# The expert products of a hybrid block: 448-column products with the two halves summed on VectorE

## Chip, cores and metric

The kernel runs on one core of one Trainium2 chip. The metric is the device time of one execution in microseconds (us).

## What is computed

One block of a hybrid network in float32 on 256 tokens of width 2048: a projection, a retention branch and an RWKV-7 branch, a gated merge, and then the layer that this change is about. It scores 16,384 experts, takes for every token 16 experts in each of 8 heads, and sums their outputs:

```
def block(args):
    xb, eb, gb = args
    ue = jnp.take(expert_u, eb, axis=0)
    act = jax.nn.gelu(jnp.einsum('nhkd,nd->nhk', ue, xb), approximate=False) * gb
    return jnp.einsum('nhk,nhkd->nd', act, jnp.take(expert_v, eb, axis=0))
...
x = x + peer(h2, peer_w_q, peer_keys_1, peer_keys_2, peer_u, peer_v)
return rms_norm(x, final_norm_w)
```

## The kernel before

224 of the 256 tokens (`DT`) are computed densely: every expert's row is multiplied with every token, and a matrix of gates `G` (128 blocks of 128 experts, by 224 tokens) is zero where an expert was not chosen. The other 32 tokens (`SPARSE`) gather their experts' rows with indirect DMAs from GpSimd and are computed on VectorE (`sparse_step`).

**Split precision.** A float32 operand is split in two parts of type fp32r: a high part (a copy on ScalarE, `hi`, L958) and a low part (raw minus high). The product is high x high, high x low activation, and low weight x high. Weights stream in as *units* of 128 x 1024, each in two halves of 512 columns. Units have four places in `raw` and two in `w_hi` and `w_lo` (`k % 2`). ScalarE makes the high part of a half when TensorE has counted `half_used` for the half four before it. The low part is made by GpSimd for the units 0 and 2 of each four (`p_split`, L1392) and by VectorE for 1 and 3 (`d_split`, L1437).

**Stage u** (64 iterations of four units, two blocks of 128 experts; `um`, L858 to L872). The two units of a block accumulate in one PSUM bank of 224 columns (bank 4 or 5). For each half: eight products of 224 columns on the high weights (high and low activation in turn, L867 and L868), then, after a wait for the low part, four on the low weights (L871). ScalarE takes Gelu from PSUM into `G` (`gelu`, L1239). VectorE picks the top 16 meanwhile, in small pieces (`pick_steps`). In the last 29 iterations (*gate turns*, i from 0 to 28) the gates are built: VectorE makes one-hot rows (`hot_e2`, `hot_e1`), ScalarE scales them (`hot_gate`, L1253), TensorE multiplies them (`gates_mm`, L879, after unit 1 and after unit 3), VectorE multiplies the result into `G` (`gate_in`, L1974) and the late Gelu results too (`late_in`, L1981). I call a half turn, two units and their gates, a *par*.

**Stage v** (64 iterations of four units; `vm`, L900 to L929). The activation of a block is split as well (ScalarE L1307, VectorE L2083, in `v_lo`), once per block, that is twice per iteration. 16 tiles of output (2048 channels) of 224 columns each stay in the eight PSUM banks, two to a bank, through the whole stage. A unit is one block and half of the output channels; again eight high products (L920) and then four low ones (L923) per half. At the end the tiles are copied to SBUF, turned (L937) and added to the residual, and the last norm follows.

The order of each engine is written out by hand: every engine runs its list in order and waits on counters. In u, VectorE and ScalarE do the work for the block before (`gelu(it - 1, ...)`) between the parts of the current one. `MAC_AT`, `DOT_AT` (when a gathered tile is used), `ADD_AT` and `FINAL_AT` are iteration numbers.

Of the kernel before, what the change touches and what calls it, by code (L numbers as in the profile page):

```python
# [102 lines left out]
def hybrid_block_kernel(nc, a):  # L103
# [4 lines left out]
    with ctx:  # L108
# [156 lines left out]
        act2 = act_both.rearrange("p c w n -> p (c w n)")[:, 0:4 * DT].rearrange("p (s w n) -> p s w n", s=2, w=2)  # L265
# [5 lines left out]
        out_T = Z(64, 80)  # L271
        part_last = small[:, 34:42].rearrange("p (t k) -> p t k", t=2)

        def v_bank(j):
            return PS[:, j // 2, (j % 2) * DT:(j % 2 + 1) * DT]

        def v_both(bank):
            return PS[:, bank, 0:2 * DT].rearrange("p (t n) -> p t n", t=2)
# [70 lines left out]
        def _(sp):  # L349
# [120 lines left out]
            def load_v(it):  # L470
                for k in range(4):
                    if isinstance(it, int) and it == 0:
                        sp.wait_ge(*split_done("u", UPAIRS - 1, k, 2))
                    else:
                        sp.wait_ge(*split_done("v", it - 1, k, 2))
                    sp.dma_start(raw[:, k, :], v_rows[ds(it * 2 + k // 2, 1), :, (k % 2) * 1024:(k % 2 + 1) * 1024]
                                 .rearrange("a e n -> e (a n)")).then_inc(S[f"raw_in{k}"], 16)
            run_loop(sp, 0, FINAL_AT, load_v)

            sp.wait_ge(S["half_used"], 2 * (V0 + 2 * 28))  # L480
            for piece in range(12):
                if piece == 8:
                    sp.wait_ge(S["rows_added"], 16 * 4)
                if piece % 2 == 0:
                    load_v(FINAL_AT + piece // 2)
                part, q = piece // 4, piece % 4
                if part == 0:
                    sp.dma_start(flat(Z(16 + 2 * q, 18 + 2 * q)),
                                 a["final_norm_w"][q * 512:(q + 1) * 512].partition_broadcast(P)).then_inc(S["fw_in"], 16)
                else:  # L490
                    tt = 2 - part
                    sp.dma_start(flat(Z(8 * tt + 2 * q, 8 * tt + 2 * q + 2)),
                                 x1_dram[tt * P:(tt + 1) * P, q * 512:(q + 1) * 512]).then_inc(S["x1_in"], 16)
            for it in range(FINAL_AT + 6, BLOCKS // 2):
                load_v(it)

            for tt in range(2):
                for h in (1, 0):
                    sp.wait_ge(*((S["normed"], 3 + tt) if h == 0 else (S["y_ready"], tt + 1)))
                    cols = slice(1024 * h, 1024 * h + 1024)  # L500
                    sp.dma_start(a["out"][0, tt * P:(tt + 1) * P, cols], flat(Z(24 + 8 * tt, 32 + 8 * tt))[:, cols]).then_inc(S["stored"], 16)
            sp.wait_ge(S["stored"], 64)
# [3 lines left out]
        def _(pe):  # L506
# [398 lines left out]
            def vm(it, k, first=False, final=False):  # L905
                b = k // 2
                if k % 2 == 0:
                    pe.wait_ge(S["act2_split"], it * 2 + (b + 1))
                for hh in range(2):
                    tiles = [(8 * (k % 2) + 4 * hh + t, slice((4 * hh + t) * P, (4 * hh + t + 1) * P)) for t in range(4)]  # L910
                    pe.wait_ge(S["unit_hi"], it * 8 + (2 * V0 + 2 * k + hh + 1))
                    for j, cols in tiles:
                        if first and j == 0:
                            pe.wait_ge(S["hot1"], 2 * GATE_TURNS)
                        if first and j in (8, 10):
                            pe.wait_ge(S[f"gelu{(j - 8) // 2}"], UPAIRS)
                        if first and j in (12, 14):
                            pe.wait_ge(S[f"gated{(j - 12) // 2}"], GATE_TURNS)
                        for w in range(2):
                            pe.matmul(v_bank(j), w_hi[:, k % 2, cols], act2[:, b, w, :], start=first and j % 2 == 0 and w == 0, stop=False)  # L920
                    pe.wait_ge(*split_done("v", it, k, hh + 1))
                    for j, cols in tiles:
                        last = pe.matmul(v_bank(j), w_lo[:, k % 2, cols], act2[:, b, 0, :], start=False, stop=final and j % 2 == 1)  # L923
                        if final and j % 2:
                            last.then_inc(S["tile_done"], 1)
                    if not final:
                        last.then_inc(S["half_used"], 1)
                    elif 2 * (k % 2) + hh > 0:
                        turn_rows(2 * (k % 2) + hh - 1)  # L929

            def turn_rows(q):

                pe.wait_ge(S["out_even"], q + 1)
                pe.wait_ge(S["out_odd"], q + 1)
                for tt in range(2):
                    for c in range(4):
                        last = pe.transpose(PS[:, 2 * q + tt, c * P:(c + 1) * P], out_T[:, 4 * q + c, tt * P:(tt + 1) * P], ident)  # L937
                    last.then_inc(S["rows_T"], 1)

            def v_pair(it, first=False, final=False):  # L940
                for k in range(4):
                    vm(it, k, first and k < 2, final and k >= 2)
            v_pair(0, first=True)
            with pe.Fori(1, BLOCKS // 2 - 1) as it:
                v_pair(it)
            v_pair(BLOCKS // 2 - 1, final=True)
            turn_rows(3)
# [3 lines left out]
        def _(act):  # L951
# [284 lines left out]
            def gelu(it, b):  # L1236

                act.wait_ge(S["half_used"], it * 8 + (2 * U0 + 4 * b + 4))
                act.activation(rowof(2 * it + b if isinstance(it, int) else it * 2 + b), PS[:, 4 + b, 0:DT], ACT.Gelu).then_inc(S[f"gelu{b}"], 1)  # L1239

            def late_gelu(i, b):

                act.wait_ge(S["half_used"], i * 8 + (2 * U0 + 8 * GATE_AT + 4 * b + 4))
                if not (isinstance(i, int) and i == 0):
                    act.wait_ge(S["late"], i * 2 + (b - 1))
                act.activation(late_out[b], PS[:, 4 + b, 0:DT], ACT.Gelu).then_inc(S[f"gelu{b}"], 1)
# [51 lines left out]
            def v_hi(it):  # L1298
                for k in range(4):
                    b = k // 2  # L1300
                    if k % 2 == 0:

                        if isinstance(it, int) and it == 0 and b == 0:
                            act.wait_ge(S["half_used"], 2 * V0 - 2)
                        else:
                            act.wait_ge(S["half_used"], it * 8 + 2 * (V0 + 2 * b - 2))
                        act.activation(act2[:, b, 0, :], rowof(2 * it + b if isinstance(it, int) else it * 2 + b), ACT.Copy).then_inc(S["act2_hi"], 1)  # L1307
                    for hh in range(2):
                        hi(it + V0 // 4, k, hh)
                    if isinstance(it, int) and it == 0 and k == 0:  # L1310
                        late_gelu(GATE_TURNS, 1)
                    if isinstance(it, int) and it == 0 and k == 1:
# [3 lines left out]
            run_loop(act, 0, EARLY // 2, v_hi)  # L1316

            act.wait_ge(S["late"], BLOCKS - EARLY)
            with act.Fori(EARLY // 2, BLOCKS // 2) as it:
                v_hi(it)  # L1320

            def odd_out(bank):
                act.wait_ge(S["tile_done"], bank + 1)
                act.activation(out_T[:, 2 * bank:2 * bank + 2, SPARSE:TOK], v_both(bank), ACT.Copy).then_inc(S["out_odd"], 1)
# [9 lines left out]
            for q in range(4):  # L1334
                odd_out(2 * q + 1)
                if q > 0:
                    square_last(0, q - 1)
                    square_last(1, q - 1)
# [12 lines left out]
        def _(pool):  # L1351
# [63 lines left out]
            for g in range(2 * UPAIRS):  # L1415
# [3 lines left out]
                if ADD_AT <= g < ADD_AT + 4:  # L1419
                    add_sparse(g - ADD_AT)  # L1420
                low_parts("u" if g < UPAIRS else "v", g % UPAIRS, U_SPLIT if g < UPAIRS else V_SPLIT, U0 // 4 + g)

# [552 lines left out]

# [212 lines left out]
```

## Time and profile before

| | |
|---|---|
| median of 3 runs | 2376.08 us (2372.18 to 2376.28) |
| profiled execution | 2374.39 us, its span 2372.6 us |
| TensorE busy | 2338.8 us, 99% of the span |
| VectorE, ScalarE, GpSimd busy | 1526.2 us, 1340.8 us, 830.7 us |
| stage u | 928.3 to 1671.0 us of the span |
| stage v | 1671.0 to 2360.1 us |
| mean granted clock of TensorE | 0.997 |

The profile gives busy time per engine, the chain of work that ended last, and groups of instructions by line with their mean duration. Products overlap in their pipeline, so an instruction's own duration (275 ns for 224 columns) says little; the distance from one start to the next is what a product costs. "Idle before" is what an engine waited for.

### The profile page before, as it was taken

The page shows a single profiled execution, that of the slowest core. Times are in us where ns is not written, and L with a number is a line of the kernel's source. Part 1 is how long each engine was busy: PE and PEld are TensorE (multiplying, and loading weights), DVE is VectorE, ACT ScalarE, POOL GpSimd, SP SyncE. Part 2 cuts the span into 40 slices and gives each one's busy share as a digit, 9 for nine tenths or more (in the row PEclk, how much of TensorE's full clock was granted, in tenths as well). Part 3 has the DMA queues.
Part 4 walks back from the last instruction along what each step waited for, and adds up shares of the span by engine and source line. Part 5 has one row for each costly group of instructions (what it writes and reads, how often), then busy time and mean ns, then how long its engine had stood idle before and what let it go on. Part 6 is the DMA issues. An engine that isn't in the chain of part 4 may idle for free.

```text
span 2372.6 us, 51129 instructions
## 1 busy us (share of the span) xinstructions
PE 2338.8 (99%) x19066; PEld 2203.6 (93%) x19066; DVE 1526.2 (64%) x2468; ACT 1340.8 (57%) x2369; POOL 830.7 (35%) x612
## 2 busy tenths in 40 slices
PE   9999999999999999999999999999999999999998
PEld 8888787978888789999999999999999999999998
DVE  5568988557566565675667877776456566666534
ACT  5456554255544545777776666666555555555555
POOL 0000201100000002445556545554556566666554
PEclk9999999999999999999999999999999999999999
DMA  7665554046666557666778766675777777777684
GB/s 215 186 195 151 160 168 152 22 128 193 194 195 215 169 182 230 193 199 220 240 260 283 255 216 233 227 242 165 259 252 248 266 248 256 260 256 262 226 256 147
DMA packets 197218, 499.52 MB, mean 211 GB/s; under 512 B 14726, under 2 KB 82824, under 8 KB 187656
## 3 DMA queue, kind: packets, MB, share of 16 engines
q1 hardware_dynamic: 187719, 430.20, 57.1%
q0 software_dynamic: 9408, 68.16, 8.2%
q8 instruction: 51, 0.84, 0.1%
q14 instruction: 40, 0.32, 0.0%
HBM read 491.98 MB, written 5.24 MB: 210 GB/s over the span
## 4 chain that ended last, share of the span: by engine, by line
PE 92%; DVE 3%; ACT 2%; DMA 1%; POOL 1%; issue 1%; SPq 0%; ACTq 0%
PE PS L920 19%; PE PS L923 10%; PE PS L518 9%; PE PS L867 9%; PE PS L868 9%; PE PS L871 9%; PE PS L561 5%; PE PS L563 5%; PE PS L562 5%; PE PS L520 4%; PE PS L511 3%; PE PS L879 2%; DVE w_lo L1437 1%; POOL big L1364 1%; DMA raw<-in_w_out 0%
## 5 line engine op out<-in xcount | busy, mean ns | idle before, releaser
L958 ACT ACTIVATE w_hi<-raw 128x512 fp32r<-128x512 f32 x1576 | 985.6, 631 | 919.9 <-PE PS L923 291.3
L1437 DVE TENSOR_TENSOR w_lo<-raw,w_hi 128x512 fp32r<-128x512 f32 x1064 | 748.3, 715 | 759.1 <-ACT w_hi L958 757.1
L1392 POOL TENSOR_TENSOR w_lo<-raw,w_hi 128x512 fp32r<-128x512 f32 x512 | 707.7, 1392 | 1095.4 <-ACT w_hi L958 1089.3
L920 PE MATMUL PS<-act_both,w_hi 128*128 128x224 f32 x4096 | 540.5, 274 | 0.0
L920 PEld LDWEIGHTS PS<-act_both,w_hi 128*128 128x128 f32 x4096 | 498.5, 192 | 0.2 <-DVE act_both L2083 0.2
L867 PE MATMUL PS<-act_both,w_hi 128*128 128x224 f32 x2048 | 489.0, 277 | 3.6 <-ACT big L1239 3.6
L868 PE MATMUL PS<-act_both,w_hi 128*128 128x224 f32 x2048 | 483.2, 274 | 0.0
L867 PEld LDWEIGHTS PS<-act_both,w_hi 128*128 128x128 f32 x2048 | 393.0, 192 | 4.3 <-issue 4.3
L868 PEld LDWEIGHTS PS<-act_both,w_hi 128*128 128x128 f32 x2048 | 393.1, 192 | 0.0
L518 PE MATMUL PS<-act_both,w_hi 128*128 128x512 f32 x1056 | 373.2, 400 | 6.9 <-DVE w_lo L1437 6.1
L923 PE MATMUL PS<-act_both,w_lo 128*128 128x224 f32 x2048 | 312.1, 275 | 0.3 <-POOL w_lo L1392 0.2
L871 PE MATMUL PS<-act_both,w_lo 128*128 128x224 f32 x2048 | 311.8, 274 | 0.0
L520 PE MATMUL PS<-act_both,w_lo 128*128 128x256 f32 x990 | 278.6, 281 | 0.0
L923 PEld LDWEIGHTS PS<-act_both,w_lo 128*128 128x128 f32 x2048 | 269.8, 192 | 0.6 <-POOL w_lo L1392 0.6
L871 PEld LDWEIGHTS PS<-act_both,w_lo 128*128 128x128 f32 x2048 | 269.8, 192 | 0.0
L518 PEld LDWEIGHTS PS<-act_both,w_hi 128*128 128x128 f32 x1056 | 197.1, 189 | 55.4 <-DVE w_lo L1437 7.9
L561 PE MATMUL PS<-w_hi,act_both 128*128 128x512 f32 x576 | 226.9, 394 | 2.5 <-DVE w_lo L1437 2.3
L563 PE MATMUL PS<-w_hi,act_both 128*128 128x512 f32 x576 | 224.2, 389 | 0.0
L562 PE MATMUL PS<-w_lo,act_both 128*128 128x512 f32 x576 | 224.2, 389 | 0.0
L520 PEld LDWEIGHTS PS<-act_both,w_lo 128*128 128x128 f32 x990 | 187.7, 190 | 1.5 <-issue 0.2
L561 PEld LDWEIGHTS PS<-w_hi,act_both 128*128 128x128 f32 x576 | 108.1, 188 | 28.0 <-DVE w_lo L1437 4.8
L563 PEld LDWEIGHTS PS<-w_hi,act_both 128*128 128x128 f32 x576 | 108.1, 188 | 22.7
(261 smaller groups left out, 1930.6 us busy)
## 6 DMA issues: line engine op xcount, KB each, us to landing
raw<-in_peer_u_t SPq DMA_DIRECT2D x256, 512.0 KB, 4.3
raw<-in_peer_v SPq DMA_DIRECT2D x256, 512.0 KB, 4.7
raw<-in_w_in SPq DMA_DIRECT2D x180, 512.0 KB, 3.8
raw<-in_w_out SPq DMA_DIRECT2D x32, 512.0 KB, 4.5
raw<-in_peer_w_q SPq DMA_DIRECT2D x32, 512.0 KB, 4.3
raw<-in_w_ret_branch SPq DMA_DIRECT2D x16, 512.0 KB, 4.4
raw<-in_w_rwkv_branch SPq DMA_DIRECT2D x16, 512.0 KB, 4.5
big<-in_x SPq DMA_DIRECT2D x2, 1024.0 KB, 5.9
```

Of the source, the lines that this page charges most:

```text
L518: last = pe.matmul(PS[:, bank, :], wh, act_both[:, kc, :, :].rearrange("p w n -> p (w n)"), start=start, stop=stop)
L520: last = pe.matmul(PS[:, bank, 0:TOK], wl, act_hi[:, kc, :], start=False, stop=False)
L561: pe.matmul(out, ah, w_hi[:, slot % 2, cols], start=first, stop=False)
L563: last = pe.matmul(out, al, w_hi[:, slot % 2, cols], start=False, stop=last_k)
L867: pe.matmul(out, w_hi[:, k % 2, cols], act_hi[:, kc, SPARSE:TOK], start=kc == 0, stop=False)
L868: pe.matmul(out, w_hi[:, k % 2, cols], act_lo[:, kc, SPARSE:TOK], start=False, stop=False)
L871: last = pe.matmul(out, w_lo[:, k % 2, cols], act_hi[:, kc, SPARSE:TOK], start=False, stop=kc == 15)
L920: pe.matmul(v_bank(j), w_hi[:, k % 2, cols], act2[:, b, w, :], start=first and j % 2 == 0 and w == 0, stop=False)
L923: last = pe.matmul(v_bank(j), w_lo[:, k % 2, cols], act2[:, b, 0, :], start=False, stop=final and j % 2 == 1)
L958: act.activation(w_hi[:, slot % 2, hh * 512:(hh + 1) * 512], raw[:, slot, hh * 512:(hh + 1) * 512], ACT.Copy).then_inc(S["unit_hi"], 1)
L1392: pool.tensor_tensor(w_lo[:, k % 2, cols], raw[:, k, cols], w_hi[:, k % 2, cols].bitcast(f32), ALU.subtract).then_inc(S["p_split"], 1)
L1437: dve.tensor_tensor(w_lo[:, slot % 2, cols], raw[:, slot, cols], w_hi[:, slot % 2, cols].bitcast(f32), ALU.subtract).then_inc(S[done], 1)
```

## The change

The two products of 224 columns on the same high weights become one of 448 (high and low activation side by side). Their results lie beside each other in PSUM, so a sum is needed: VectorE's `tensor_reduce` over the pair. In u that is `usum`, one for each of the 128 blocks, ahead of Gelu, which now reads and writes SBUF. In v, 448 columns take a whole bank for each tile, so only eight of the 16 tiles fit: stage v runs twice over all 128 blocks, each time for half of the channels (`h` = 0, 1), with a drain between (`last_units`, `sum_tile`, `odd_out`); a unit is then one block, and its activation is split in both passes. The long and the short product of each piece of 128 columns come in turn, and the wait for the low part stands ahead of both. Some iteration numbers move with it, and the last rows are turned in another grouping (`rows_of`).

```diff
             def um(it, k):
-                out = PS[:, 4 + k // 2, 0:DT]
+                bank = 4 + k // 2
                 for hh in range(2):
                     if k % 2 == 0 and hh == 0:
-                        wait_past(pe, S[f"gelu{k // 2}"], it)
-                    pe.wait_ge(S["unit_hi"], it * 8 + (2 * U0 + 2 * k + hh + 1))
+                        wait_past(pe, S[f"gelu{k // 2}"], 2 * it - 1)
+                    pe.wait_ge(*split_done("u", it, k, hh + 1))
                     chunks = [((k % 2) * 8 + 4 * hh + c, slice((4 * hh + c) * P, (4 * hh + c + 1) * P)) for c in range(4)]
                     for kc, cols in chunks:
-                        pe.matmul(out, w_hi[:, k % 2, cols], act_hi[:, kc, SPARSE:TOK], start=kc == 0, stop=False)
-                        pe.matmul(out, w_hi[:, k % 2, cols], act_lo[:, kc, SPARSE:TOK], start=False, stop=False)
-                    pe.wait_ge(*split_done("u", it, k, hh + 1))
-                    for kc, cols in chunks:
-                        last = pe.matmul(out, w_lo[:, k % 2, cols], act_hi[:, kc, SPARSE:TOK], start=False, stop=kc == 15)
+                        pe.matmul(pair_bank(bank), w_hi[:, k % 2, cols], act_both[:, kc, :, SPARSE:TOK], start=kc == 0, stop=False)
+                        last = pe.matmul(PS[:, bank, 0:DT], w_lo[:, k % 2, cols], act_hi[:, kc, SPARSE:TOK], start=False, stop=kc == 15)
                     last.then_inc(S["half_used"], 1)
...
             def late_gelu(i, b):
-                act.wait_ge(S["half_used"], i * 8 + (2 * U0 + 8 * GATE_AT + 4 * b + 4))
...
-                act.activation(late_out[b], PS[:, 4 + b, 0:DT], ACT.Gelu).then_inc(S[f"gelu{b}"], 1)
+                act.wait_ge(S[f"gelu{b}"], 2 * i + (2 * GATE_AT + 1))
+                act.activation(late_out[b], late_out[b], ACT.Gelu).then_inc(S[f"gelu{b}"], 1)
...
+            def usum(it, b, late=True):
+                dve.wait_ge(S["half_used"], it * 8 + (2 * U0 + 4 * b + 4))
+                dve.tensor_reduce(late_out[b] if late else G[:, 2 * it + b, :], summed(4 + b), AX.X, ALU.add).then_inc(S[f"gelu{b}"], 1)
...
                 for par in range(2):
+                    usum(i + (GATE_AT - 1), par, not first)
                     if not first:
                         gate_in(i - 1, par)
...
+            def v_lo(h, it):
+                g = UPAIRS + h * (BLOCKS // 4) + it
+                for k in range(4):
...
+                    dve.wait_ge(S["act2_hi"], it * 4 + (h * BLOCKS + k + 1))
+                    dve.tensor_tensor(act2[:, k, 1, :], rowof(4 * it + k), act2[:, k, 0, :].bitcast(f32), ALU.subtract).then_inc(S["act2_split"], 1)
...
-MAC_AT = [66 + 8 * t // 5 for t in range(PICK_TILES)]
+MAC_AT = [66 + 8 * t // 5 for t in range(17)] + [100 + 5 * t // 4 for t in range(PICK_TILES - 17)]
...
-IDS_AT, ADD_AT, FINAL_AT = 15, 118, 54
+IDS_AT, ADD_AT, FINAL_AT = 15, 119, 24
```

The order of instructions shows what moves. TensorE, one half of a unit of stage u, before:

```order
L867 MATMUL PS<-act_both,w_hi 128x224 [waits s_unit_hi]
L868 MATMUL PS<-act_both,w_hi 128x224
L867 MATMUL PS<-act_both,w_hi 128x224
L868 MATMUL PS<-act_both,w_hi 128x224
L871 MATMUL PS<-act_both,w_lo 128x224 [waits s_p_split]
L871 MATMUL PS<-act_both,w_lo 128x224 x3
```

and changed, where L876 is the long product and L877 the short one:

```order
L876 MATMUL PS<-act_both,w_hi 128x448 [waits s_p_split]
L877 MATMUL PS<-act_both,w_lo 128x224
L876 MATMUL PS<-act_both,w_hi 128x448
L877 MATMUL PS<-act_both,w_lo 128x224
```

Eight and four products of 224 columns have become four of 448 and four of 224, and the half waits for its low part before its first product and not before its ninth. (Of the eight high products the first piece shows four.)

VectorE, one par of a gate turn with a gathered tile, before (L1437 are the low parts, L2002 the gathered tile):

```order
L1974 TENSOR_TENSOR big<-PS,big 128x128x4 [waits s_late,s_g_mm1]
L1986 TENSOR_TENSOR onehot<-PS,extra 128x512 [waits s_g_mm1]
L1989 TENSOR_TENSOR cst<-PS,extra 128x512
L1981 TENSOR_TENSOR big<-big,extra 128x224 [waits s_gated1,s_gelu1]
L1437 TENSOR_TENSOR w_lo<-raw,w_hi 128x512 [waits s_unit_hi] x2
L2002 ISA big,vec<-big,inv 128x1024
```

and changed (L1485 and L2055 are the low parts and the gathered tile there):

```order
L2027 TENSOR_REDUCE extra<-PS 128x224 [waits s_half_used]
L2022 TENSOR_TENSOR big<-PS,big 128x128x4 [waits s_late,s_g_mm1]
L2039 TENSOR_TENSOR onehot<-PS,extra 128x512 [waits s_g_mm1]
L2042 TENSOR_TENSOR cst<-PS,extra 128x512
L2034 TENSOR_TENSOR big<-big,extra 128x224 [waits s_gated1,s_gelu1]
L1485 TENSOR_TENSOR w_lo<-raw,w_hi 128x512 [waits s_unit_hi] x2
L2055 ISA big,vec<-big,inv 128x1024
L2027 TENSOR_REDUCE cst<-PS 128x224 [waits s_half_used]
```

The sum of a block stands at the head of a par, behind the low parts and the gathered tile of the par before. ScalarE, changed, from the last high part of one par to the next par (L1277 is the late Gelu, L1284 the scaling of the one-hot rows):

```order
L990 ACTIVATE w_hi<-raw 128x512 [waits s_half_used]
L1277 ACTIVATE extra<-extra 128x224 [waits s_gelu1]
L1284 ACTIVATE cst<-cst,extra 128x128 [waits s_hot0]
L1284 ACTIVATE cst<-cst,extra 128x128 x3
L990 ACTIVATE w_hi<-raw 128x512 [waits s_half_used,s_raw_in2]
```

The order is that of before; the Gelu's wait was on TensorE's counter `half_used` and is now on the sum (`s_gelu1` counts sums and Gelus).

## Rows read from the trace of the kernel before

**Rows 1.** The page: busy time of the engines, and the chain that ended last by engine and line.

```profile
PE 2338.8 (99%) x19066; PEld 2203.6 (93%) x19066; DVE 1526.2 (64%) x2468; ACT 1340.8 (57%) x2369; POOL 830.7 (35%) x612
...
PE 92%; DVE 3%; ACT 2%; DMA 1%; POOL 1%; issue 1%; SPq 0%; ACTq 0%
```

**Rows 2.** Windows: u without gates, gate turns, v, the end.

```profile
928.40:1313.00 384.60, 380.98 (x3394) 380.27 (x3394) 261.31 (x649) 283.42 (x427) 204.74 (x156) 1.00 0.72 231
1313.00:1662.00 349.00, 349.00 (x3128) 349.00 (x3127) 257.43 (x414) 219.06 (x501) 174.40 (x129) 1.00 0.67 223
1671.00:2354.00 683.00, 682.73 (x6110) 682.21 (x6109) 375.09 (x451) 358.02 (x641) 400.89 (x290) 1.00 0.73 248
2354.00:2372.60 18.60, 8.03 (x71) 7.57 (x70) 11.26 (x21) 9.66 (x24) 4.70 (x2) 0.81 0.28 113
```

**Rows 3.** Chain in order of time (start, us, what), stage v, one half of a unit.

```profile
2345.84 0.45 PE PS L923 x4
2346.29 0.89 PE PS L920 x8
2347.18 0.45 PE PS L923 x4
```

**Rows 4.** The same view in the query projection: 512 and 256 columns in turn.

```profile
879.26 0.23 PE PS L518
879.49 0.12 PE PS L520
879.61 0.24 PE PS L518
```

**Rows 5.** Timeline of TensorE: products of 512 columns alone; and the chain's turns of 128 columns.

```profile
599.84 0.39 PE L563 MATMUL PS<-w_hi,act_both 128*128 128x512 f32 x1
600.07 0.39 PE L561 MATMUL PS<-w_hi,act_both 128*128 128x512 f32 x1
600.29 0.39 PE L562 MATMUL PS<-w_lo,act_both 128*128 128x512 f32 x1
...
2357.88 0.87 PE PS L937 x8
```

**Rows 6.** Timeline of a gate turn, TensorE's two groups of gate products.

```profile
1453.12 1.06 PE L879 MATMUL PS<-cst 128*128 128x128 f32 x8
1459.37 1.06 PE L879 MATMUL PS<-cst,onehot 128*128 128x128 f32 x8
```

**Rows 7.** Timeline of the same turn, VectorE.

```profile
1454.59 0.68 DVE L1974 TENSOR_TENSOR big<-PS,big 128x512 f32<-128x512 f32 x1
...
1456.38 1.42 DVE L1981 TENSOR_TENSOR big<-big,cst 128x224 f32<-128x224 f32 x1
...
1460.23 0.69 DVE L1437 TENSOR_TENSOR w_lo<-raw,w_hi 128x512 fp32r<-128x512 f32 x1 [0.65 <-ACT w_hi L958]
1460.84 1.22 DVE L2002 CUSTOM_DVE_ANT_0 inv<-inv 128x1024 f32<-128x1024 f32 x1
1461.99 0.08 DVE L2002 DVE_READ_ACCUMULATOR2_ANT vec<- 128x1 f32 x1
1461.99 0.68 DVE L1974 TENSOR_TENSOR big<-PS,big 128x512 f32<-128x512 f32 x1
```

**Rows 8.** Timeline of the same turn, ScalarE and GpSimd.

```profile
1459.57 0.63 ACT L958 ACTIVATE w_hi<-raw 128x512 fp32r<-128x512 f32 x1 [0.71 <-PE PS L871]
1460.11 0.34 ACT L1246 ACTIVATE extra<-PS 128x224 f32<-128x224 f32 x1
1460.35 1.27 ACT L1253 ACTIVATE cst<-cst,extra 128x128 f32<-128x128 f32 x4
...
1456.26 2.69 POOL L1392 TENSOR_TENSOR w_lo<-raw,w_hi 128x512 fp32r<-128x512 f32 x2 [2.10 <-ACT w_hi L958]
```

**Rows 9.** One line's instructions, min/median/max ns: a PSUM copy of 448, and the activation's low part.

```profile
L2104 DVE COPY big<-PS x4: 617/625/625, 2354.3 to 2359.9; 128x448 f32<-128x448 f32 x4
...
L2083 DVE TENSOR_TENSOR act_both<-big,act_both x128: 327/392/1487, 1669.2 to 2348.9; 128x224 fp32r<-128x224 f32 x128
```

**Rows 10.** Timeline of ScalarE in u without gates.

```profile
1100.18 1.28 ACT L1239 ACT_TABLE_LOAD   x1
1101.47 0.36 ACT L1239 ACTIVATE big<-PS 128x224 f32 x1
1101.72 1.14 ACT L958 ACTIVATE w_hi<-raw 128x512 fp32r<-128x512 f32 x2
```

**Rows 11.** Who waited for whom in stage v: us in total, times, longest; and a weight load's landing.

```profile
ACT w_hi L958 <- PE PS L923: 291.3, 464, 1.1
...
ACT w_hi L958 <- DMA raw<-in_peer_v: 31.3, 22, 1.9
...
raw<-in_peer_v SPq DMA_DIRECT2D x256, 512.0 KB, 4.7
```

More of the change, by code:

```diff
@@ L909, in vm @@
+            def vm(h, it, k, first=False):
+                pe.wait_ge(S["act2_split"], it * 4 + (h * BLOCKS + k + 1))
                 for hh in range(2):
-                    tiles = [(8 * (k % 2) + 4 * hh + t, slice((4 * hh + t) * P, (4 * hh + t + 1) * P)) for t in range(4)]
-                    pe.wait_ge(S["unit_hi"], it * 8 + (2 * V0 + 2 * k + hh + 1))
+                    tiles = [(4 * hh + t, slice((4 * hh + t) * P, (4 * hh + t + 1) * P)) for t in range(4)]
+                    pe.wait_ge(*split_done("v", it + h * (BLOCKS // 4), k, hh + 1))
@@ L912, in vm @@
                     for j, cols in tiles:
[L913 to L929, printed above, removed]
@@ L931, in turn_rows @@
-            def turn_rows(q):
-                pe.wait_ge(S["out_even"], q + 1)
-                pe.wait_ge(S["out_odd"], q + 1)
-                for tt in range(2):
+                        if first:
+                            bank_free(h, j)
+                        pe.matmul(pair_bank(j), w_hi[:, k % 2, cols], act2[:, k], start=first, stop=False)
+                        last = pe.matmul(PS[:, j, 0:DT], w_lo[:, k % 2, cols], act2[:, k, 0, :], start=False, stop=False)
+                    last.then_inc(S["half_used"], 1)
@@ L938, in turn_rows, with last_units @@
                     last.then_inc(S["rows_T"], 1)
[L940 to L947, printed above, removed]
+            def last_units(h):
+                it = BLOCKS // 4 - 1
+                for j in range(8):
+                    cols, halves = slice(j * P, (j + 1) * P), j // 4 + 1
+                    for k in (2, 3):
+                        if j == 0:
+                            pe.wait_ge(S["act2_split"], h * BLOCKS + 4 * it + k + 1)
+                        if j % 4 == 0:
+                            pe.wait_ge(S["unit_hi"], 2 * (V0 + h * BLOCKS + 4 * it + k) + halves)
+                        pe.matmul(pair_bank(j), w_hi[:, k % 2, cols], act2[:, k], start=False, stop=False)
+                    for k in (2, 3):
+                        if j % 4 == 0:
+                            pe.wait_ge(*split_done("v", it + h * (BLOCKS // 4), k, halves))
+                        last = pe.matmul(PS[:, j, 0:DT], w_lo[:, k % 2, cols], act2[:, k, 0, :], start=False, stop=k == 3)
+                        if k == 2 and j % 4 == 3:
+                            last.then_inc(S["half_used"], 1 if j == 3 else 3)
+                    last.then_inc(S["tile_done"], 1)
+                    if h == 1 and j in (2, 4, 6):
+                        turn_rows((j - 2) // 2)
+                if h == 1:
+                    turn_rows(3)
@@ L950, in _, with v_blocks @@
+            for h in range(2):
+                def v_blocks(it, first=False, final=False):
+                    for k in range(2 if final else 4):
+                        vm(h, it, k, first and k == 0)
+                    if final:
+                        last_units(h)
+                v_blocks(0, first=True)
+                with pe.Fori(1, BLOCKS // 4 - 1) as it:
+                    v_blocks(it)
+                v_blocks(BLOCKS // 4 - 1, final=True)
         @block.scalar
@@ L1315, in v_hi @@
                         sqrt_table()
-            run_loop(act, 0, EARLY // 2, v_hi)
+                    if start and h == 1 and k == 0:
+                        odd_out(7)
+            run_loop(act, 0, EARLY // 4, lambda it: v_hi(0, it))
             act.wait_ge(S["late"], BLOCKS - EARLY)
[L1319 to L1324, printed above, removed]
+            with act.Fori(EARLY // 4, BLOCKS // 4) as it:
+                v_hi(0, it)
+            run_loop(act, 0, BLOCKS // 4, lambda it: v_hi(1, it))
             def square_last(tt, q):
@@ L2032, in u_step @@
                     sparse_step(it, k // 2)
+                if unit >= 4 and k % 2 == 0:
+                    usum(it - 1, k // 2, False)
             def scale_rows(w):
@@ L2076, in _ @@
                 gate_turn(i)
[L2077 to L2089 removed]
+            usum(BLOCKS // 2 - 1, 0)
```

202 lines of the change are left out of this document (121 added, 81 removed).

## The prediction

> **What bounds the kernel now.** I read the page first. TensorE is busy 99% of the span and the chain that ended last runs on it for 92% [rows 1], so the kernel is as long as TensorE's list. The windows then say where the change acts: 384.6 us of stage u without gates, 349.0 us of gate turns, 683.0 us of stage v, TensorE busy throughout [rows 2]. The change touches these three. What is read next is the distance between products, since overlapping durations do not show it.
>
> One half of a unit takes 0.89 us for its eight high products and 0.45 us for its four low ones [rows 3], so 1.34 us for twelve, 0.112 us each, and three products, the work on one piece of 128 weight columns, take 0.335 us. The turns, with 128 columns, take 0.87 us for eight, 0.109 us each [rows 5]. So a product of 224 columns costs hardly more than one of 128: at this width it is not the columns that set the distance but what comes with every product, the load of its own weights.
>
> **What a long product costs.** No product of 448 columns is in the trace. The nearest rows are 512 and 256 columns in turn, 0.235 and 0.118 us, 0.353 for the pair [rows 4], and 512 alone, 0.227 us [rows 5]. The bounds for 448 with 224:
> - Below, in proportion to the columns: 0.353 x 672 / 768 = 0.309 us. That gains 0.026 on 0.335.
> - Above, the short one as in rows 4 (0.118) and the long one less 64 columns at the 0.4 to 0.46 ns per column of rows 4 and 5, 0.207: 0.325 us, a gain of 0.010.
> - I take 0.207 + 0.112 = 0.319 us, because the short product is most like those of 224 columns in rows 3, and no product there or in rows 5 comes in less than 0.109. Gain 0.016 us.
>
> There are 128 blocks x 16 pieces in u and as many in v, 4,096 pieces: 66 us of TensorE's time (41 to 106). A half is then 4 x 0.319 = 1.28 us instead of 1.34, and an iteration of eight halves 10.21 instead of 10.72, 0.51 less.
>
> The Trainium skill (TensorE: Matmul & The Clock Gate, section LDWEIGHTS) gives a weight load as the columns divided by 1.2, 107 ns for 128; the 109 to 112 ns of rows 3 and 5 agree. The same page (Back-to-back issue gap) gives an isolated product as N/2.4 + 2.5 ns. That would make the long one 189 ns and the pair with a load of 107 come to 296, a gain of 160 us over the pieces; but by it 512 columns would take 216 ns, and the trace has 227.
>
> **What the sum adds, and what now stands behind it.** A copy of 448 columns from PSUM takes VectorE 0.62 us [rows 9]; I take that for the sum. Next to instructions of 0.68 us that follow at 0.60 us [rows 7] it occupies some 0.6.
>
> *Gate turns* (28 with gates, 56 pars; a par now takes 1459.37 - 1453.12 = 6.25 us [rows 6]). TensorE alone would need 4 x 1.28 + 0.90 = 6.01. But ScalarE's late Gelu waits for a sum that VectorE issues behind the low parts and the gathered tile of the par before. The loop from one last high part to the next: low part 0.61 (1460.23 to 1460.84), gathered tile 1.15 (to 1461.99) [rows 7], sum 0.62, Gelu 0.24 and scaling 1.27 [rows 8], four high parts at 0.57 to 0.63, which TensorE does not hold up then, 2.4 [rows 8, 10]: 6.3 us. With handovers 6.35. It needs no TensorE, so where a gathered tile is used (20 of the 29 turns, by `DOT_AT`) it sets the par: 6.35 instead of 6.25, 40 x 0.10 = +4 us. In the other 16 pars, without the 1.15, the loop is 5.2 and TensorE sets 6.01: -4 us. To that comes a collision: VectorE's `late_in` took 1.42 us where GpSimd's low part had begun just before (1456.26 and 1456.38 [rows 7, 8]). The sum pushes `late_in` to about 1.8 us behind itself, and GpSimd starts its low part some 2.2 us behind it, so now one waits, now the other; I put down 5 us. Gate turns: +5, all in all nothing won. This is the first place where the gain stays out.
>
> *u without gates* (35 iterations): -0.51 x 35 = -18 us. Here the loop after the last high part of an iteration is low part 0.69, perhaps a gathered tile 1.2, a piece of the top-16 work of 1 to 1.8, sum 0.62, and then ScalarE's table load 1.28 and Gelu 0.36 [rows 10], which start only when the sum is done, high part 0.6, low part 0.7. That is 7.2 us at most against six halves less one high part, 7.0 us, until TensorE needs it. So it bites in the six iterations that have both a gathered tile and top-16 work, and more weakly elsewhere: 5 us, and 3 us for weights that land late, which the wait ahead of the first product no longer forgives. -18 + 8 = -10.
>
> *Stage v* (64 iterations): -0.51 x 64 = -33 us. Added are 128 activation splits: ScalarE 0.37 us, VectorE 0.33 to 1.49 [rows 9]. VectorE is busy 375 of 683 us and ScalarE 358 [rows 2]; with 128 x 0.9 = 115 and 128 x 0.37 = 47 us more both stay under 75% of the shorter stage, and they are split a unit ahead, so they cost nothing while these engines keep two microseconds of lead. The wait ahead costs lead: the high part of a half starts when the half four before it is done, and its low part from GpSimd is there 0.1 + 0.6 + 1.4 = 2.1 us later; TensorE wants it after three halves, 3.8 us. Spare is 1.7 us, where today the low part had 3.9 + 0.9 - 2.1 = 2.8. ScalarE waited for weights 22 times, 1.4 us in the mean, 1.9 at most [rows 11], and the window in which a load must land (4.7 us in the middle) shrinks by 0.4 us. I put down 5 us for it, 1 for the drain between the two passes (the first half of the new pass waits for the last tiles), 2 for the end, where eight sums of 0.62 us lie beside the adds. -33 + 8 = -25.
>
> The exclusive port behind the spread of rows 9 is in the Trainium skill (SBUF — State Buffer, Who interferes with whom): VectorE with two SBUF inputs and a GpSimd instruction that reads SBUF block each other for a whole instruction, a `tensor_reduce` never does. The maximum of 1487 ns against a minimum of 327 agrees. It speaks against the 128 new splits, and not against the sums; by it the sum would change only if the splits' lead were gone.
>
> **Sum.** -10 + 5 - 25 = -30 us on 2374.4, so 2344; the median of the runs shown lies 1.7 above the profiled execution, so 2346.
>
> **Rivals.**
> - *Columns alone set the distance* (0.309 us a piece). For it: rows 4 are nearly in proportion (0.235 to 0.118). Against: rows 5 and 3, where 128 columns cost what 224 do. u without gates -32 + 9, gate turns as above but 16 pars at 5.84 (-7 + 9), v -54 + 12 = -42, so -63 and 2313 us. Chance 0.23.
> - *The lead is worth as much as the gain.* If each late load shows in full and there are twice as many, 44 x 1.4 = 62 us is more than v gains; halved, it takes 25 to 30 us: 2372 us, no change or little. For it: the lead of 1.7 us is under the longest wait of 1.9 [rows 11]. Against: the mean is under it, and VectorE's units have 0.7 us more. Chance 0.18.
> - *Slower: ScalarE's list hangs on the sum in every gate par.* If `late_in` meets GpSimd each time, it takes 1.42 instead of 0.38 [rows 7], the low parts come 1.0 us later, and the loop is 7.4 us in the 40 pars with a tile. That is +46 us against -35 from the rest: 2387 us. It decides from a mean par of 6.25 + 35/56 = 6.87 us on. For it: the loop already fills the par by my count. Against: the trace shows the short and the long `late_in` both. Chance 0.17.
> - *The change doesn't do what it says.* The order shows the 448-column products, the sums and the waits as written, so I give it 0.02.
>
> **Chances.** My case 0.40, and the rest as said. A measurement of this kernel tells about 0.2%, 4.8 us, from no change. The first two cases are faster, of the third about half: 0.74. Within 0.2%: 0.08. Slower: the fourth and a little of the third, 0.18. The range must reach into the first and the last rival: 2308 to 2380.
>
> **What the changed profile would show.** The pair of L876 and L877 at 0.319 us, 0.309 or 0.325 decides between the first two cases. The gate products' groups 6.35 us apart in turns with a tile and 6.0 without. ScalarE's waits for VectorE's L2027 in gate turns, of the order of a microsecond each. TensorE idle, now next to nothing in u and v, by some 20 us, in the low parts' name. I would be wrong if a pair took 0.33 us or more, if the sum took over a microsecond, or if TensorE stood in stage v for more than the 22 late loads.

## The result and the profile after

| | before | changed |
|---|---|---|
| median | 2376.08 us (2372.18 to 2376.35, 5 runs) | 2391.24 us (2387.59 to 2396.62, 5 runs) |
| span of the profiled execution | 2372.6 us | 2389.2 us |
| TensorE busy | 99% | 96% |
| VectorE busy | 1526 us | 1801 us |
| mean granted clock | 0.997 | 0.996 |

The change is slower: ratio 1.0071, 95% interval 1.0059 to 1.0083. I had forecast 2346 us, in a range of 2308 to 2380.

The page of the changed kernel, busy time and the chain, against [rows 1]:

```profile
PE 2290.7 (96%) x14970; PEld 2059.2 (86%) x14970; DVE 1801.1 (75%) x2731; ACT 1355.7 (57%) x2497; POOL 856.6 (36%) x616
...
PE 62%; DVE 20%; ACT 8%; issue 4%; DMA 2%; POOL 2%; ACTq 1%; SPq 0%; DVEq 0%
```

The chain was 92% TensorE. Now a fifth of it is VectorE, and ScalarE has 8%. The windows, cut at the same places as in [rows 2] (u without gates, gate turns, v, the end; the columns are busy time of TensorE's products, its loads, VectorE, ScalarE, GpSimd):

```profile
929.50:1306.50 377.00, 359.48 (x2250) 335.39 (x2248) 294.97 (x715) 276.21 (x422) 206.09 (x155) 1.00 0.72 234
1306.50:1699.40 392.90, 357.42 (x2237) 320.33 (x2238) 331.32 (x470) 204.42 (x505) 186.96 (x129) 1.00 0.55 197
1710.00:2366.00 656.00, 642.17 (x4064) 607.60 (x4063) 533.82 (x582) 395.29 (x772) 411.38 (x295) 1.00 0.78 260
2366.00:2389.20 23.20, 10.21 (x69) 8.78 (x67) 14.64 (x27) 8.43 (x22) 4.90 (x3) 0.80 0.26 90
```

From the starts of the products the stages come out as follows. The span grew by 16.6 us, which is the sum of the differences within a microsecond:

| stage | before | changed | difference | forecast |
|---|---|---|---|---|
| ahead of stage u | 928.4 | 929.5 | +1.1 | 0 |
| u without gates, 35 iterations | 381.8 | 377.0 | -4.8 | -10 |
| the other 29 iterations, with the gate turns | 360.2 | 403.4 | +43.2 | +5 |
| v, first to last long product | 688.3 | 664.8 | -23.5 | -27 |
| the end | 13.2 | 14.1 | +0.9 | +2 |

The products themselves did what they should. The chain in order of time, stage v, a long product (L930) and a short one (L931) in turn, against [rows 3, 4]:

```profile
1730.54 0.21 PE PS L930
1730.75 0.10 PE PS L931
1730.85 0.21 PE PS L930
1731.06 0.10 PE PS L931
1731.16 0.21 PE PS L930
```

0.62 us for two pieces (one long product and one short), and over all pieces the medians of the distances are 0.213 and 0.101 us in v, 0.211 and 0.104 in u. From the start of one half to the next, where nothing stalls, it is 1.253 us for four pieces, against 1.340 before. A piece takes 0.313 us, a little less than my 0.319, and an undisturbed iteration 10.03 us where it took 10.72 in v and 10.76 in u.

The loss is in the gate turns. One par of the changed kernel follows, in the timelines of ScalarE, VectorE and GpSimd, to be held against [rows 7, 8] (L2027 is the sum, L1277 the late Gelu, L1284 the scaling, L990 a high part, L1485 and L1434 low parts, L2055 the gathered tile):

```profile
1443.67 0.40 ACT L1277 ACTIVATE cst<-cst 128x224 f32<-128x224 f32 x1 [3.75 <-DVE cst L2027]
1443.97 1.27 ACT L1284 ACTIVATE cst<-cst,extra 128x128 f32<-128x128 f32 x4
1445.14 2.17 ACT L990 ACTIVATE w_hi<-raw 128x512 fp32r<-128x512 f32 x4
1451.06 0.39 ACT L1277 ACTIVATE extra<-extra 128x224 f32<-128x224 f32 x1 [3.74 <-DVE extra L2027]
```

```profile
1443.03 0.61 DVE L2027 TENSOR_REDUCE cst<-PS 128x224 f32<-128x448 f32 x1
...
1445.36 0.37 DVE L2034 TENSOR_TENSOR big<-big,cst 128x224 f32<-128x224 f32 x1
1446.83 2.51 DVE L1485 TENSOR_TENSOR w_lo<-raw,w_hi 128x512 fp32r<-128x512 f32 x2 [1.10 <-ACT w_hi L990]
1449.26 1.21 DVE L2055 CUSTOM_DVE_ANT_0 big<-big,inv 128x1024 f32<-128x1024 f32 x1
...
1450.41 0.61 DVE L2027 TENSOR_REDUCE extra<-PS 128x224 f32<-128x448 f32 x1
```

```profile
1445.84 2.95 POOL L1434 TENSOR_TENSOR w_lo<-raw,w_hi 128x512 fp32r<-128x512 f32 x2 [3.04 <-ACT w_hi L990]
```

From sum to sum it is 7.38 us (1443.03 to 1450.41). ScalarE stands 3.7 us in each par for the sum; then it issues four high parts in a row, for which it used to wait one by one on TensorE. GpSimd takes its two at once, 1445.84 to 1448.79. VectorE's two low parts start in this time, at 1446.83, and take 2.51 us together, against 0.69 each in [rows 7]. Taken one by one they are 0.82 and 1.77 us, and GpSimd's two are 1.27 and 1.73 us. The times fit engines that take turns: VectorE's first gets in between GpSimd's two, and its second gets through only when GpSimd's second is done. Tile, sum and Gelu wait behind them. It is the same in nearly every par. VectorE's low parts over all gate turns, before and changed (one line's instructions, min/median/max ns):

```profile
L1437 DVE TENSOR_TENSOR w_lo<-raw,w_hi x112: 674/693/718, 1316.4 to 1660.3; 128x512 fp32r<-128x512 f32 x112
```

```profile
L1485 DVE TENSOR_TENSOR w_lo<-raw,w_hi x112: 678/1066/1775, 1306.5 to 1693.8; 128x512 fp32r<-128x512 f32 x112
```

TensorE, which needs 5.9 us for a par (experiment 2), is in none of these steps. The waits of the whole stretch of gate turns (us in total, times, longest):

```profile
ACT cst L1277 <- DVE cst L2027: 94.8, 28, 3.8
ACT extra L1277 <- DVE extra L2027: 92.1, 27, 3.8
```

Theory A, after the result, is this loop with the collision of low parts in it. Theory B: VectorE has too much work in a gate turn, so that the sum costs as work and not as a wait. Theory C: the wait for the low part ahead of the long products costs.

### The profile page after: what moved, and what is told of

Same layout as the page of the kernel before. It is cut to its first block, busy times and chain, and to the rows that moved or that the text cites. A ratio compares the mean times of both kernels' runs of the same rounds, so it can differ in the third digit from the quotient of the medians.

```text
span 2389.2 us, 42796 instructions
## 1 busy us (share of the span) xinstructions
PE 2290.7 (96%) x14970; PEld 2059.2 (86%) x14970; DVE 1801.1 (75%) x2731; ACT 1355.7 (57%) x2497; POOL 856.6 (36%) x616
## 4 chain that ended last, share of the span: by engine, by line
PE 62%; DVE 20%; ACT 8%; issue 4%; DMA 2%; POOL 2%; ACTq 1%; SPq 0%; DVEq 0%
PE PS L930 15%; PE PS L527 9%; DVE w_lo L1485 9%; PE PS L931 7%; PE PS L570 5%; PE PS L572 5%; PE PS L571 5%; ACT w_hi L990 5%; PE PS L529 4%; PE PS L876 4%; PE PS L520 3%; DVE big L2055 2%; PE PS L877 2%; ACT cst L1284 2%; POOL w_lo L1434 1%
## 5 line engine op out<-in xcount | busy, mean ns | idle before, releaser
L990 ACT ACTIVATE w_hi<-raw 128x512 fp32r<-128x512 f32 x1576 | 957.9, 628 | 656.5 <-PE PS L931 238.9
L1434 POOL TENSOR_TENSOR w_lo<-raw,w_hi 128x512 fp32r<-128x512 f32 x512 | 739.9, 1466 | 1073.3 <-ACT w_hi L990 1073.0
L1485 DVE TENSOR_TENSOR w_lo<-raw,w_hi 128x512 fp32r<-128x512 f32 x1064 | 801.2, 774 | 396.7 <-ACT w_hi L990 393.2
L876 PE MATMUL PS<-act_both,w_hi 128*128 128x448 f32 x2048 | 664.2, 379 | 53.1 <-POOL w_lo L1434 40.7
L930 PE MATMUL PS<-act_both,w_hi 128*128 128x448 f32 x2016 | 635.4, 376 | 13.8 <-DVE act_both L2147 7.4
L877 PE MATMUL PS<-act_both,w_lo 128*128 128x224 f32 x2048 | 543.2, 265 | 0.0
L931 PE MATMUL PS<-act_both,w_lo 128*128 128x224 f32 x2016 | 532.1, 264 | 0.0
L876 PEld LDWEIGHTS PS<-act_both,w_hi 128*128 128x128 f32 x2048 | 383.8, 187 | 111.8 <-POOL w_lo L1434 73.1
L930 PEld LDWEIGHTS PS<-act_both,w_hi 128*128 128x128 f32 x2016 | 378.1, 188 | 48.0 <-POOL w_lo L1434 13.3
L877 PEld LDWEIGHTS PS<-act_both,w_lo 128*128 128x128 f32 x2048 | 390.1, 190 | 0.0
L931 PEld LDWEIGHTS PS<-act_both,w_lo 128*128 128x128 f32 x2016 | 384.6, 191 | 0.0
L2147 DVE TENSOR_TENSOR act_both<-big,act_both 128x224 fp32r<-128x224 f32 x256 | 279.8, 1113 | 102.9 <-ACT act_both L1345 102.9
L527 PEld LDWEIGHTS PS<-act_both,w_hi 128*128 128x128 f32 x1056 | 197.1, 189 | 55.3 <-DVE w_lo L1485 7.9
L529 PEld LDWEIGHTS PS<-act_both,w_lo 128*128 128x128 f32 x990 | 187.8, 190 | 1.5 <-issue 0.2
L571 PEld LDWEIGHTS PS<-w_lo,act_both 128*128 128x128 f32 x576 | 108.2, 188 | 22.4 <-issue 0.5
```

Source lines behind the costliest of these rows:

```text
L527: last = pe.matmul(PS[:, bank, :], wh, act_both[:, kc, :, :].rearrange("p w n -> p (w n)"), start=start, stop=stop)
L529: last = pe.matmul(PS[:, bank, 0:TOK], wl, act_hi[:, kc, :], start=False, stop=False)
L571: pe.matmul(out, ah, w_lo[:, slot % 2, cols], start=False, stop=False)
L876: pe.matmul(pair_bank(bank), w_hi[:, k % 2, cols], act_both[:, kc, :, SPARSE:TOK], start=kc == 0, stop=False)
L877: last = pe.matmul(PS[:, bank, 0:DT], w_lo[:, k % 2, cols], act_hi[:, kc, SPARSE:TOK], start=False, stop=kc == 15)
L930: pe.matmul(pair_bank(j), w_hi[:, k % 2, cols], act2[:, k], start=first, stop=False)
```

## Experiments

All are made from the changed kernel. Times are medians with their ratio to the kernel before on the same chip.

**1. The sum ahead of the gathered tile, in gate turns.**

```diff
                 for par in range(2):
-                    usum(i + (GATE_AT - 1), par, not first)
+                    if first and par == 0:
+                        usum(GATE_AT - 1, 0, False)
...
                             u_lo(i + GATE_AT, k)
+                    if par == 0:
+                        usum(i + (GATE_AT - 1), 1, not first)
+                    else:
+                        usum(i + GATE_AT, 0)
                     sparse_step(i + GATE_AT, par)
...
-            usum(BLOCKS // 2 - 1, 0)
```

> The change with, in gate turns, the sum of a block moved ahead of the gathered tile on VectorE (low parts, sum, tile instead of low parts, tile, sum). Theory A (a loop through low part, tile 1.15 us, sum, Gelu, scaling, four high parts and GpSimd's two low parts sets the par at 7.38 us): the 1.15 us leaves the loop, pars with a tile fall to about 6.3 us, 40 x 1.1 = 44 us gained, about 2347 us; the tile now fills time in which VectorE waited 1.1 us. Theory B (VectorE has too much work in gate turns: the sum counts as work, wherever it stands): no change against the changed kernel, 2391 us. Theory C (the wait for the low part ahead of the long products is what costs): no change, 2391 us.

Measured: 2359.07 us, ratio 0.9932 (0.9916 to 0.9949); the mean distance between gate products fell from 7.04 to 6.45 us. 32 us of the expected 44 came, with no work taken away. A sum that costs as work, and a wait ahead of the long products, would both have stayed. So B and C are out for the most part, and VectorE's order matters.

**2. The late Gelu behind the next unit's high parts.**

```diff
-                    if k == 1:
-                        if not (isinstance(i, int) and i == 0):
-                            late_gelu(i - 1, 1)
-                        if not last:
-                            hot_gate(i, 0)
-                    if k == 3:
-                        late_gelu(i, 0)
-                        if not last:
-                            hot_gate(i, 1)
+                    elif k % 2 == 0:
+                        late_gelu(i - 1, k // 2)
+                    if k % 2 and not last:
+                        hot_gate(i, k // 2)
...
+                        late_gelu(GATE_TURNS, 0)
```

> The change with, in gate turns, ScalarE's late Gelu moved behind the next unit's two high parts; all engines do the same work. Theory A: ScalarE no longer holds the high parts of unit 0 and 2 back for the sum, GpSimd's low parts start earlier and TensorE sets the par at 4 x 1.26 + 0.90 = 5.9 to 6.1 us; 40 pars x 1.3 + 16 x 0.3 = 57 us gained, about 2335 us, faster than the kernel before. Theory B (VectorE's work, about 6.3 us in a par with a tile): little gained, 2380 to 2391 us. Theory C: no change, 2391 us.

Measured: 2326.57 us, ratio 0.9799 (0.9782 to 0.9815). Two gate-product groups in succession, timeline of TensorE of this kernel:

```profile
1443.24 1.06 PE L885 MATMUL PS<-cst,onehot 128*128 128x128 f32 x8
1449.14 1.06 PE L885 MATMUL PS<-cst 128*128 128x128 f32 x8
```

and its windows, gate turns and v:

```profile
1305.00:1642.00 337.00, 337.00 (x2282) 323.73 (x2281) 305.07 (x475) 224.90 (x507) 163.28 (x133) 1.00 0.70 233
1643.00:2308.00 665.00, 650.23 (x4120) 614.83 (x4118) 541.78 (x594) 397.35 (x777) 410.58 (x295) 1.00 0.76 255
```

All 55 distances are 5.9 us and TensorE is busy for all of the 337 us, with VectorE at 305, as many instructions as ever. The only thing moved is the late Gelu in ScalarE's list, once in each par. That shows the loop of A and refutes B: 63 of the 64.7 us between this kernel and the changed one are in the gate iterations (403.4 to 340.6). GpSimd's pair takes 2.55 us there and meets `late_in` (0.9 to 1.3 us), for which TensorE does not wait, and not the low parts (0.68 us each). What the collision is worth within the loop is not shown by this run but by experiments 5 and 6.

**3. The low part waited for behind the long products.**

```diff
                     for kc, cols in chunks:
                         pe.matmul(pair_bank(bank), w_hi[:, k % 2, cols], act_both[:, kc, :, SPARSE:TOK], start=kc == 0, stop=False)
+                    pe.wait_ge(*split_done("u", it, k, hh + 1))
+                    for kc, cols in chunks:
                         last = pe.matmul(PS[:, bank, 0:DT], w_lo[:, k % 2, cols], act_hi[:, kc, SPARSE:TOK], start=False, stop=kc == 15)
```

and the same in v; ahead of the long products stands the wait for the high part.

> The change with the low part waited for only behind the four long products of a half, then the four short ones, in u and v (but for the last units of a pass). Theory A: gate turns stay at 7.38 us a par (the loop has no TensorE in it); the stalls of u without gates (about 10 us) and of v (about 15 us) shrink by half or more: 2378 us, if the products cost the same in this order. Theory C: gate turns recover too, 2335 to 2350 us. Theory B: no change, 2391 us. Products grouped by kind: 0.314 us for a long and a short one if the order does not matter.

Measured: 2392.02 us, ratio 1.0075 (1.0057 to 1.0092), the changed kernel's time. The par is 7.07 us in the mean, u without gates 377.7 us, v 2.0 us shorter. C is out as the cause of the loss: the gate turns did not recover. But two things cancel outside them. Four long products took 0.82 us and four short ones 0.44 in v, 1.260 us for a half where it is 1.253 in turn, and an undisturbed iteration of u took 10.13 us and not 10.03. By these distances the grouped order costs some 7 us in u without gates and v together (an estimate). What is left of these two stages beyond their undisturbed halves fell by 3 and by 6 us. So the wait ahead of both products costs some 8 us, of A's side expectation of 13, and this edit pays nearly as much for the order.

**4. Stage v alone.** Stage u as in the kernel before: `um`, `gelu`, `late_gelu` and `late_in`'s count taken from there, `usum` out.

> Stage u as in the kernel before (three products of 224 columns, Gelu from PSUM, no sums), stage v as changed. Theories A and B: v alone gains about 24 us, so 2352 us; everything lost is in u. Theory C: v pays for its wait too and gains less than 10 us: 2366 us or more.

Measured: 2355.13 us, ratio 0.9913 (0.9889 to 0.9937). Its u took 381.8 and 360.2 us, as before, its v 669.0 us, within 5 of the changed kernel's. So v gains some 20 us by itself, and all that was lost was lost in u.

**5. GpSimd reads nothing.** From the first gate turn on GpSimd fills the low parts of its units with zeros, so the low parts of half the weights are left out.

```diff
+                        if m >= U0 // 4 + GATE_AT:
+                            pool.memset(w_lo[:, k % 2, cols].bitcast(f32), 0.0).then_inc(S["p_split"], 1)
+                            continue
                         pool.tensor_tensor(w_lo[:, k % 2, cols], raw[:, k, cols], w_hi[:, k % 2, cols].bitcast(f32),
```

> The change, but from the first gate turn on GpSimd fills its units' low parts with zeros instead of subtracting, so the low parts of half the expert weights are left out; it reads no SBUF. Theory A with a collision (VectorE's low part stands until both of GpSimd's are done, which is the 1.0 us that the prediction missed in the loop): a par with a tile falls from 7.38 to about 6.2 us, and in v the gathered tiles of 3 to 4 us fall to 1.3 and the stalls of about 2 us at some iterations with them. Rival (the loop is that long for the order alone): 7.3 us still.

Measured: 2314.61 us in one timing. The loop is still there, ScalarE still waits for the sum, but the par is 5.9 us mostly and 6.2 at most, and v takes 648.1 us, 16.7 less than in the changed kernel. The gathered tiles in v, of the changed kernel and of this one (one line's instructions, min/median/max ns):

```profile
L2062 DVE SCALAR_TENSOR_TENSOR big<-inv,vec,big x42: 1268/1273/3965, 1744.4 to 2268.1; 128x1024 f32<-128x1024 f32 x42
```

```profile
L2065 DVE SCALAR_TENSOR_TENSOR big<-inv,vec,big x42: 1275/1279/1282, 1684.4 to 2191.2; 128x1024 f32<-128x1024 f32 x42
```

The memsets are also quicker (two in 1.05 us against 2.95), so this alone does not tell reads from time.

**6. GpSimd writes slowly.** As 5, in 16 pieces for each half.

```diff
-                            pool.memset(w_lo[:, k % 2, cols].bitcast(f32), 0.0).then_inc(S["p_split"], 1)
+                            for n in range(16):
+                                last = pool.memset(w_lo[:, k % 2, hh * 512 + 32 * n:hh * 512 + 32 * n + 32].bitcast(f32), 0.0)
+                            last.then_inc(S["p_split"], 1)
```

> As e9_gpsimd_reads_nothing (low parts of GpSimd's units left out, zeros in their place), but the zeros are written in 16 pieces for each half, so that GpSimd takes about as long as it does to subtract or longer, and still reads no SBUF. Theory A (VectorE's two-input instructions are held while GpSimd reads): VectorE's low parts stay at 0.69 us, the gathered tiles of v at 1.28, the par well under 7.38 us although GpSimd is as slow. Rival (GpSimd's time, not its reads, made the loop long): the par goes back to 7 us or more, the low parts of VectorE to 1.3 in the mean.

Measured: 2319.61 us in one timing. The two halves took GpSimd 1.98 us, twice as long as in 5 and still less than when it subtracts, so the test is not as sharp as meant. VectorE, with GpSimd under way from 1443.73 to 1445.71:

```profile
1444.74 0.69 DVE L1490 TENSOR_TENSOR w_lo<-raw,w_hi 128x512 fp32r<-128x512 f32 x1 [1.10 <-ACT w_hi L990]
1445.76 0.69 DVE L1490 TENSOR_TENSOR w_lo<-raw,w_hi 128x512 fp32r<-128x512 f32 x1 [0.33 <-ACT w_hi L990]
```

```profile
1443.73 1.98 POOL L1436 MEMSET w_lo<- 128x32 f32 x32 [3.04 <-ACT w_hi L990]
```

The first low part began in the middle of GpSimd's writes and took its 0.69 us, and all 64 tiles of v took 1.28 us. The mean par is 6.03 us, 6.19 at most, and v took 649.1 us. In these runs an overlap with a GpSimd that writes costs VectorE nothing, and an overlap with one that reads holds it back. The Trainium skill (SBUF — State Buffer, Who interferes with whom) says just this of an instruction with two SBUF inputs; the 0.69 us here and the 2.51 us for two above agree.

**7. The Gelu a unit later in all of u.** As 2, and in `u_blocks` the Gelu stands at `k % 2` and not at `k % 2 == 0`.

> As e2_gelu_behind_high_parts, and in u without gates too ScalarE's Gelu stands one unit later (behind the high parts of units 1 and 3, not 0 and 2). Theory A (a wait for the sum in ScalarE's list is what costs in all of u): u without gates falls from 375 us towards 35 x 10.03 = 351, at least 10 us gained on e2: 2316 us or less. Theory D (there it is VectorE's order, low parts behind top-16 work and tile, that holds the products up): no more than 3 us gained.

Measured: 2317.89 us, ratio 0.9761 (0.9745 to 0.9778). u without gates went from 375.2 us in experiment 2 to 366.8 us, 8.4 and not 24: a third was ScalarE's wait, the rest is not. The iterations that stay long are single ones (12.6 us at the 25th, 10.8 to 11.2 from the 28th on).

**8. The sum directly behind the low parts in all of u.** As 7, with `usum` ahead of the tile and the top-16 work.

> As e6, and the sum stands directly behind VectorE's low parts and ahead of the gathered tile and the top-16 work in all of u. Theory A: little beyond e6, since the wait is gone already, 0 to 4 us. Theory D: a gain beyond e6 as TensorE waits for a bank until its sum is done: 5 us or more. Gate turns stay at 5.9 us a par by both.

Measured: 2325.97 us, ratio 0.9799 (0.9783 to 0.9816), slower than experiment 7 by 8 us, all of it in u without gates (374.9 us). Both theories expected no loss. The two traces point to the same collision: in u without gates eight gathered tiles took 1.8 to 2.2 us, where one did in 7, and in the iteration that grew most, from 10.1 to 14.2 us, VectorE's two low parts took 3.43 us together, having started 0.06 us behind a pair of GpSimd's. No further run was made to show it.

**9. The low wait once more, without the loop.** 7 and 3 together.

> As e6_gelu_late_everywhere (no wait for the sum in front of the high parts), with the four long products of a half ahead of the wait for its low part, as in e4. Theory A: with the loop gone the lead of a half is 1.7 us and the order of the wait matters only at late loads, 0 to 6 us gained on e6 or nothing, 2312 to 2319 us. Theory C (the wait ahead of both is a cost of its own, hidden in e4 by the loop): 10 us or more gained on e6.

Measured: 2324.89 us, ratio 0.9787 (0.9770 to 0.9803), 7 us over experiment 7 by the medians, with intervals that just touch. The two effects of experiment 3 are here too: a par takes 5.96 us for 5.91 and an undisturbed iteration of u 10.13 for 10.03, while the stalls of u without gates and of v are each some 3 us less. To wait late behind grouped products gains nothing in this kernel, with the loop or without it. An order that waits late and still takes the products in turn was not tried.

**10. The gathered tile ahead of the low parts in v.** As 7, `sparse_step` behind the splits of units 0 and 2.

> As e6_gelu_late_everywhere, and in v the gathered tile stands behind the activation split of units 0 and 2, ahead of the low parts, and not behind the low parts of units 1 and 3. Theory A (v loses some 20 us because a tile that comes late falls behind a pair of GpSimd's low parts and takes 3.96 us): VectorE is done with the tile before GpSimd starts its pair, the tiles of more than 2 us go and v gains 5 to 15 us, 2303 to 2313 us. Rival: a late load does it whatever the tile's place: no change, 2318 us.

Measured: 2316.81 us, ratio 0.9748 (0.9731 to 0.9764), not to be told from 7. The mechanism expected did not come about either: 36 of 64 tiles now took over 2 us, where it was 7, and still v took 2.7 us less. So a long tile does not by itself cost TensorE time in v. What made these harmless is not shown; it may be that nothing urgent follows them now, and this trace also has more late loads (27 of ScalarE's waits, 47.4 us, against 19 and 24.2 in 7).

## Why the prediction was wrong

*What a long product costs*: right, 0.313 us a piece for 0.319, though the floor of 0.112 under a short product was wrong (0.101 to 0.104 in turn with a long one). The gain in TensorE's own time, over 1,024 halves of 1.253 for 1.340 us, is 89 us, not 66.

*Gate turns*: this step failed. The loop was found and so was the fact that TensorE is not in it, but it was priced at 6.35 us and took 7.38, in 38 of the 55 distances; without a tile nearly all were 6.25 to 6.27 and not 6.01. The term that failed is four high parts and a low part, 2.4 + 0.61 = 3.0 us. From the first high part to the end of the low parts it is 4.1 us (1445.14 to 1449.26). The other terms held: 2.1 us for sum, Gelu and scaling, 1.15 for the tile. I had seen a collision of this size in [rows 7, 8], as `late_in`'s 1.42 us, and put it down as "now one waits, now the other", 5 us in all. `late_in` does not collide at all (0.37 us). What collides, in nearly every par, are VectorE's low parts. I had copied the four high parts as 2.4 us and gone on to VectorE's low part at 0.61, without asking what a ScalarE that issues four high parts at once sets off: GpSimd runs its two back to back, 2.95 us, over the place where VectorE's come. So +43 stood where I had +5. That is 38 of the 45 us between 2346 and 2391; most of the rest is the two stages below.

*The third rival* had the price of the loop, 7.4 us, and the time, 2387 us, from the wrong instruction. By its point of decision, a mean par of 6.87 us, it is the rival that came true in the time (7.04 measured), by luck and not by its mechanism. It had a chance of 0.17, too little for a loop that by my own count already filled the par. My judgement now: a loop that just fits, with a collision open that is worth a sixth of it, is an even bet and not a correction of 5 us.

*u without gates*: the gain per iteration was larger than forecast (10.03 us, so 26 us for 35 iterations) and the stalls too, 21 us for 8. The chain that I named is there (experiment 7), for a third of it. That -4.8 lies so near to -10 is luck: both terms were off, and the errors cancel for the most part.

*Stage v*: 23.5 us for 27, again with both terms larger and errors that cancel: 44 us gained on the products, 21 lost. I took the activation splits as free, but their median is now 1.34 us and the longest 3.35 (0.39 and 1.49 in [rows 9]), and they too stand beside GpSimd's reads. Late loads, my term for the loss, did not grow: 16 waits, 18.5 us, against 22 and 31.3 in [rows 11]. In experiments 5 and 6 17 and 16 of the 21 us went, though in 5 late loads made 28.5 us of waits. What share of this is the reads is open: in both runs GpSimd's low parts are also done sooner, and in the changed kernel TensorE and its weight loads stood 17.3 us in v for GpSimd's low parts and 9.8 us for the activation splits. (The lead of before in the prediction, 3.9 + 0.9 - 2.1, is 2.7 us and not 2.8; nothing hangs on it.)

```profile
L2147 DVE TENSOR_TENSOR act_both<-big,act_both x256: 376/1340/3349, 1708.4 to 2365.1; 128x224 fp32r<-128x224 f32 x128
```

*The wait ahead of both products* cost some 8 us in u without gates and v, by experiment 3, which is what the prediction had for it (3 and 5). It had no part in the loss of the gate turns.

## What to carry to other kernels

When the result of one engine goes through a second before a third may go on, look for the loop that closes without the busiest engine, and price it with everything that runs beside it once that engine no longer paces it: what used to arrive one by one then arrives at once. Such a loop is often broken by moving one short instruction behind those that others wait for: here one Gelu turned +0.7% into -2.0%, and a second into -2.4%. Products of 448 columns in place of two of 224 took 6.5% off a half here (1.340 to 1.253 us), where nothing stalls.

## What the runs showed of the hardware

Products of 128 and of 224 columns stand 0.11 us apart when each size runs by itself, but 224 columns behind 448 take 0.101 to 0.104. Four pairs took 1.253 us in turn, and 1.260 in v and 1.266 in the mean in u when grouped by length.

A VectorE instruction with two SBUF inputs can be held for two GpSimd instructions in a row that read SBUF, 3.96 us for one of 1.28. Such a case in v of the changed kernel, a gathered tile beside two low parts of GpSimd's:

```profile
1801.24 3.96 DVE L2062 SCALAR_TENSOR_TENSOR big<-inv,vec,big 128x1024 f32<-128x1024 f32 x1
```

```profile
1801.56 2.55 POOL L1434 TENSOR_TENSOR w_lo<-raw,w_hi 128x512 fp32r<-128x512 f32 x2
```

In a gate turn the two engines' low parts went in turns (0.82 and 1.77 us on VectorE, 1.27 and 1.73 on GpSimd). GpSimd's writes did not hold VectorE back (0.69 us in the middle of them).
